# Closing residual sum and RMSNorm of a diffusion trunk: the sums on VectorE alone, Ln and Exp per pair of tiles, three tiles scaled by GpSimd

## The reference, cut to what matters

```python
def rmsnorm(x, g):
    xf = x.astype(jnp.float32)
    y = xf * lax.rsqrt(jnp.mean(xf * xf, axis=-1, keepdims=True) + EPS)
    return (y * g.astype(jnp.float32)).astype(x.dtype)

# expert_choice_ffn
ys = jnp.einsum('becf,efd->becd', hid, w_down) * gates[..., None].astype(h.dtype)
return jnp.zeros_like(h).at[bidx, idx].add(ys)

# trunk_layer, its last step
x = x + gate2 * expert_choice_ffn(h, router_w, exp_w_gate, exp_w_up, exp_w_down)

# at the end
y_prompt = rmsnorm(xp, final_norm_g)
y_sample = rmsnorm(xs, final_norm_g)
```

## Time and profile before

| what | value |
|---|---|
| median of three executions | 2427.76 us (2424.95 to 2427.86) |
| the profiled execution's own time | 2428.42 us |
| its span in the trace | 2426.7 us |
| PE busy | 2327.6 us (96%) |
| DVE busy | 1107.5 us (46%) |
| ACT busy | 937.2 us (39%) |
| POOL busy | 379.9 us (16%), 267 instructions |
| granted TensorE clock, mean | 0.984 |

### The profile page before, as it was taken

One profiled execution on the slowest core, in us unless ns is written; L12 is line 12 of the kernel. 1 busy time (PEld: TensorE's weight loads), 2 busy tenths in 40 slices (PEclk: granted clock), 3 DMA queues, 4 the chain that ended last, 5 costly groups with the idle time before them and its releaser, 6 DMA issues.

```text
span 2426.7 us, 39841 instructions
## 1 busy us (share of the span) xinstructions
PE 2327.6 (96%) x14256; PEld 1695.5 (70%) x14256; DVE 1107.5 (46%) x2161; ACT 937.2 (39%) x2447; POOL 379.9 (16%) x267
## 2 busy tenths in 40 slices
PE   6989999999999999999999999679999999999998
PEld 3456666575656565665644444579999999999996
DVE  2577786868686776766235317710010001000013
ACT  3164646556473747454311133213222322223213
POOL 0241313223140314132100000000010100110010
PEclk8999999999999999999999999889999999999999
DMA  9521212020211112121442422458778887888874
GB/s 343 219 58 38 69 37 68 17 88 18 64 42 41 56 28 68 28 69 40 149 169 95 143 89 94 161 211 295 267 251 282 291 296 241 270 287 294 283 233 159
DMA packets 198403, 361.06 MB, mean 149 GB/s; under 512 B 8955, under 2 KB 72328, under 8 KB 195244
## 3 DMA queue, kind: packets, MB, share of 16 engines
q1 hardware_dynamic: 192139, 341.77, 40.3%
q0 software_dynamic: 6176, 18.29, 3.0%
HBM read 319.97 MB, written 40.06 MB: 148 GB/s over the span
## 4 chain that ended last, share of the span: by engine, by line
PE 86%; DVE 5%; issue 3%; ACT 3%; DMA 2%; DVEq 0%; SPq 0%; ACTq 0%; POOL 0%; POOLq 0%
PE bank L757 22%; PE bank L2426 21%; PE bank L2440 11%; PE bank L2055 5%; PE bank L1792 5%; PE bank L957 3%; PE bank L1810 2%; PE bank L735 2%; PE bank L949 2%; PE bank L1015 2%; PE bank L1026 1%; PE bank L1031 1%; DMA arena<-in_ada_w 1%; PE bank L743 1%; PE bank L1030 1%
## 5 line engine op out<-in xcount | busy, mean ns | idle before, releaser
L757 PE MATMUL bank<-arena 128*128 128x512 f32 x1344 | 678.1, 608 | 2.8 <-ACT arena L791 2.8
L2426 PE MATMUL bank<-arena 128*128 128x144 f32 x4096 | 513.1, 286 | 3.1 <-ACT arena L2474 3.1
L2426 PEld LDWEIGHTS bank<-arena 128*128 128x128 f32 x4096 | 509.8, 190 | 3.2 <-ACT arena L2474 3.2
L2541 DVE TENSOR_TENSOR arena<-arena,bank 128x144 f32<-128x144 f32 x128 | 39.2, 306 | 700.2 <-ACT arena L2488 700.2
L757 PEld LDWEIGHTS bank<-arena 128*128 128x128 f32 x1344 | 217.8, 191 | 91.9 <-issue 87.5
L2440 PE MATMUL bank<-arena 128*128 128x144 f32 x2048 | 257.3, 286 | 0.7 <-DVE arena L2541 0.7
L2440 PEld LDWEIGHTS bank<-arena 128*128 128x128 f32 x2048 | 253.8, 189 | 1.9 <-DVE arena L2541 0.9
L2488 ACT ACTIVATE arena<-bank 128x144 f32<-128x144 f32 x128 | 37.5, 293 | 464.4 <-PE bank L2426 464.4
L957 PEld LDWEIGHTS bank<-arena 128*128 128x128 f16 x1296 | 96.4, 98 | 156.0 <-issue 137.4
L1135 ACT ACTIVATE arena<-bank 128x384 f16<-128x384 f16 (+1 forms) x360 | 159.4, 490 | 92.1 <-PE bank L957 67.5
L791 ACT ACTIVATE arena<-bank 128x128 f32<-128x128 f32 (+1 forms) x156 | 75.9, 491 | 172.4 <-PE bank L757 107.9
(11 more groups left out here) (309 smaller groups left out, 3213.5 us busy)
## 6 DMA issues: line engine op xcount, KB each, us to landing
arena<-in_exp_w_gate SPq DMA_DIRECT2D x32, 2048.0 KB, 10.0
arena<-in_exp_w_up SPq DMA_DIRECT2D x32, 2048.0 KB, 15.0
arena<-in_exp_w_down SPq DMA_DIRECT2D x32, 2048.0 KB, 10.8
arena<-in_w_in SPq DMA_DIRECT2D x52, 512.0 KB, 5.3
arena<-in_ada_w SPq DMA_DIRECT2D x24, 1024.0 KB, 7.9
side_dram<-arena SPq DMA_DIRECT2D x20, 576.0 KB, 4.4
arena<-g_dram SPq DMA_DIRECT2D x16, 576.0 KB, 4.1
arena<-in_x_sample SPq DMA_DIRECT2D x16, 512.0 KB, 7.2
```

The source lines that it names most:

```text
L757: ins = nc.tensor.matmul(bank[:, 0:LH], w[:, k, :], x[:, k, :], start=(k == 0 and job[2] in "127"), stop=(k == KH - 1), skip_group_check=( ...
L2426: last = nc.tensor.matmul(banks[3 + f % 2][:, m * CAP:(m + 1) * CAP], w_unit[2 * half + m][:, k, col:col + P], xsT[:, k, :], start=(k == 0 ...
```

## The change

1. `BY_TENSOR` goes. All nine sums are made by VectorE; TensorE has no identity matmuls left in this stage (L2460, 8 of its 48 matmul rows of this stage), ScalarE no copies from PSUM.
2. Ln and Exp run once per group of `LAST_GROUPS` = (0,1), (2,3), (4,5), (6,7), (8), over one or two columns, after the Squares of the whole group; `rstd2` counts groups. ScalarE also waits for its own previous step before each Square.
3. VectorE's order is: the sums of a group, then the scales of the group before it.
4. Tiles 1, 3 and 6 (`BY_POOL`) are scaled by GpSimd in two operations, a tensor_scalar with `frs` and then a tensor_tensor with `fin_row`, with a wait for the first between them. The stores of these tiles wait for GpSimd; the order of the stores stays.

```diff
@@ pe9
-            whole = i in BY_TENSOR
-            if whole:
-                pe.wait_ge(sem(f"tile_in{i}"), 16 + 16)
-                for half in range(2):
-                    nc.tensor.matmul(pair[half][:, 0:512], ident, xf[i][:, half * 512:(half + 1) * 512], start=True, stop=False)
...
-                    last = nc.tensor.matmul(pair[half][:, 0:512], place_l[:, i - 1, :], ys_l[:, half * 512:(half + 1) * 512], start=not whole, stop=True)
+                    last = nc.tensor.matmul(pair[half][:, 0:512], place_l[:, i - 1, :], ys_l[:, half * 512:(half + 1) * 512], start=True, stop=True)
-    BY_TENSOR = (2, 5)
+    LAST_GROUPS = ((0, 1), (2, 3), (4, 5), (6, 7), (8,))
+    BY_POOL = (1, 3, 6)
@@ sync10
-            sp.wait_ge(sem("yf_ready"), t + 1)
+            if t in BY_POOL:
+                sp.wait_ge(sem(f"tile_in{t}"), 16 + 16 + 2)
+            else:
+                sp.wait_ge(sem("yf_ready"), t + 1 - sum(b < t for b in BY_POOL))
@@ act10
+        for group in LAST_GROUPS:
+            at, to = group[0], group[-1] + 1
+            for t in group:
+                act.wait_ge(sem("x_summed"), t + 1)
+                act.wait_ge(sem("act_step"), n)
+                nc.scalar.activation(sqf, xf[t], ACT.Square, accum_out=fss[:, t:t + 1]).then_inc(sem("act_step"), 1)
+                n += 1
+            act.wait_ge(sem("act_step"), n)
+            nc.scalar.activation(fln[:, at:to], fss[:, at:to], ACT.Ln, scale=1.0 / D, bias=eps_c).then_inc(sem("act_step"), 1)
             n += 1
             act.wait_ge(sem("act_step"), n)
+            nc.scalar.activation(frs[:, at:to], fln[:, at:to], ACT.Exp, scale=-0.5).then_inc(sem("rstd2"), 1)
@@ dve10
-        def scale(t):
-            dve.wait_ge(sem("rstd2"), NT + t + 1)
-            nc.vector.scalar_tensor_tensor(xf[t], xf[t], frs[:, t:t + 1], fin_row, ALU.mult, ALU.mult).then_inc(sem("yf_ready"), 1)
...
+        def scale(n):
+            dve.wait_ge(sem("rstd2"), NT + n + 1)
+            for t in LAST_GROUPS[n]:
+                if t not in BY_POOL:
+                    nc.vector.scalar_tensor_tensor(xf[t], xf[t], frs[:, t:t + 1], fin_row, ALU.mult, ALU.mult).then_inc(sem("yf_ready"), 1)
+
+        for n, group in enumerate(LAST_GROUPS):
+            for t in group:
+                add(t)
+            if n > 0:
+                scale(n - 1)
+        scale(len(LAST_GROUPS) - 1)
+
+    def pool10(pool):
+        pool.wait_ge(sem("rows_in"), ROWS_ALL + 16)
+        for n, group in enumerate(LAST_GROUPS):
+            pool.wait_ge(sem("rstd2"), NT + n + 1)
+            for t in group:
+                if t in BY_POOL:
+                    pool.wait_ge(sem(f"tile_in{t}"), 16 + 16)
+                    nc.gpsimd.tensor_scalar(xf[t], xf[t], frs[:, t:t + 1], None, ALU.mult).then_inc(sem(f"tile_in{t}"), 1)
+                    pool.wait_ge(sem(f"tile_in{t}"), 16 + 16 + 1)
+                    nc.gpsimd.tensor_tensor(xf[t], xf[t], fin_row, ALU.mult).then_inc(sem(f"tile_in{t}"), 1)
```

More of the change, by code:

```diff
@@ L2608, in act10 @@
         n = ACT_PRO + 2 * NT
[L2609 to L2616, removed]
+        for group in LAST_GROUPS:
[7 more added lines that the diff above has]
+            nc.scalar.activation(fln[:, at:to], fss[:, at:to], ACT.Ln, scale=1.0 / D, bias=eps_c).then_inc(sem("act_step"), 1)
             n += 1
-            nc.scalar.activation(sqf, xf[t], ACT.Square, accum_out=fss[:, t:t + 1]).then_inc(sem("act_step"), 1)
             act.wait_ge(sem("act_step"), n)
[L2620 to L2623, removed]
+            nc.scalar.activation(frs[:, at:to], fln[:, at:to], ACT.Exp, scale=-0.5).then_inc(sem("rstd2"), 1)
     def dve10(dve):
@@ L2628, in add @@
         def add(t):
-            if t in BY_TENSOR:
-                return
             dve.wait_ge(sem(f"tile_in{t}"), 16 + 16)
             dve.wait_ge(sem("y_filled"), NT + t + 1)
-            if t - 1 in BY_TENSOR:
-                dve.wait_ge(sem("x_summed"), t)
             pair = PAIRS[t % len(PAIRS)]
@@ L2699, in f_pool @@
             pool9(pool)
+            pool10(pool)
     return {"sync": f_sync, "tensor": f_pe, "scalar": f_act, "vector": f_dve, "gpsimd": f_pool}
```

## The result

The changed kernel took 2429.76 us in the median of 18 runs (2428.0 to 2433.84), the kernel before 2426.71 us in the median of its 18 (2424.95 to 2429.72). The ratio is 1.0015, with a 95% interval of 1.0008 to 1.0021: a small loss of 3.1 us, with an interval of 1.9 to 5.1 us. The 3.1 us lie inside the 0.2%, or 4.9 us, that was called no change. The profiled execution of the changed kernel took 2430.77 us with a span of 2429.1 us, 2.4 us over the span before.

What follows compares the result with a forecast made beforehand. The closing stage was taken as bound by VectorE's sums and scales, with contention from GpSimd deciding. The middle of plus 1.3 and plus 2.8 us, plus 2.0, on a base of 2427.8 gave 2429.8 us, range 2425.0 to 2433.2.

Steps and rivals of the forecast that it cites:

- signs written down for a wrong forecast: Closing stage: a scale at 1.28 us across a GpSimd operation, a tensor_scalar over 2 us, or tile 6 stored after VectorE's last scale.
- Without contention VectorE would end at 2420.4: VectorE's new order with nothing held: scale 8 runs from 2419.1 to 2420.4, 3.1 us ahead of before.
- Sums go free, GpSimd's operations and scales exclude each other: Port rule: VectorE's scales and GpSimd's operations block each other for their full length; sums from PSUM are not held.
- The tensor_scalar takes 1.1 us: GpSimd's first operation per tile, 1024 columns: 1.1 us, taken nearest to the affine_selects.
- The end that I kept, 3.1: Upper end for GpSimd's tensor_scalar: the one row of 1.55 us for 512 columns, doubled to 3.1 us.
- two estimates of 0.9 and 2.2 us: GpSimd's operations with one and two inputs over 1024 elements, by the Trainium skill's cycles per element at 1.2 GHz.
- Scale 0 held by 1.9 us, scale 2 by 0.9, then scale 7 or 8 by 2.2: VectorE's scales behind GpSimd's operations: scale 0 1.9 us late, scale 2 2.8 us late in all, scale 8 ending at 2424.7 or 2424.8.
- the second rival: GpSimd slower than taken: with a 3.1 us tensor_scalar, stores pile up, plus 6.9 us, 2434.7; chance 0.23.
- The first to start wins, scales 4 and 5 run before GpSimd gets its turn: Order on the port: scales 4 and 5 run until 2418.9, and only then tile 6's tensor_scalar, to 2419.9.
- The stores of 6, 7 and 8 pile up if GpSimd is second: If scale 7 beats tile 6's tensor_tensor, the stores land 1.28 us apart, the last at 2428.9: 2.8 us later.
- the other (plus 1.3): If tile 6's tensor_tensor beats scale 7, scale 8 ends at 2424.7 and the last store lands at 2427.4, 1.3 us later.
- The gain on TensorE is only a bound: TensorE fills tile 8 at 2413.7 instead of 2417.2, 3.4 us, counting only as long as VectorE waits for TensorE.

Runs made afterwards that it cites:

- e8: Changed kernel without GpSimd's tensor_tensor, tiles 1, 3 and 6 stored without the gains; one execution, VectorE ends 22.6 us after TensorE's first placing matmul.
- e2: Changed kernel with the gains copied to PSUM for VectorE's scales, done in two halves, and three bank pairs for sums; ratio to the kernel before 1.0001.
- e4: Kernel before plus, after its last store, thirteen probes of GpSimd operations alone or beside VectorE's scales or sums; tensor_scalar alone 2.85 us, tensor_tensor alone 2.34 us.
- e7: Changed kernel without GpSimd's tensor_scalar, tiles 1, 3 and 6 stored without 1/rms; one execution, VectorE ends 23.5 us after TensorE's first placing matmul.
- e9: Changed kernel with the stores of tiles 6 and 7 exchanged; last packet at 29.2 us after TensorE's first placing matmul, ratio to the kernel before 1.0006.
- e3: Kernel before with BY_TENSOR empty, so VectorE makes all sums, nothing else changed; ratio to the kernel before 1.0004, VectorE ends at 25.0 us.
- e1: Changed kernel with BY_POOL empty, so all sums and scales on VectorE in the new order; ratio to the kernel before 0.9999, VectorE ends at 25.5 us.
- e10: Changed kernel with tile 6 scaled by VectorE again, GpSimd keeping tiles 1 and 3; ratio to the kernel before 0.9999, VectorE ends at 25.3 us.

## Why the prediction was right, point by point

The number was right, and so was the core of the mechanism: scales held behind GpSimd, and stores piled up behind tile 6. But the steps that led to it were wrong in the length of the tensor_scalar, in what it holds, in who wins and so in which scales are held, and they cancelled. That they did was luck. Two of the signs written down for a wrong forecast came true, a scale at 1.28 us across a GpSimd operation (tile 0) and a tensor_scalar over 2 us, and the scales of tiles 0 and 2 took 1.28 and 1.37 us, not 3.1 and 2.2.

That 2429.8 met 2429.76 is luck as well. The change was forecast as plus 2.0 us and measured as plus 3.1; the base, 2427.8 from three executions, was 1.1 us above the 2426.71 of eighteen.

- *Without contention VectorE would end at 2420.4.* Right: e8, with no scale held, ends 22.6 us after the first placing matmul, which is 2420.4.
- *Sums go free, GpSimd's operations and scales exclude each other.* Right for the sums and, once it has got its turn, for the tensor_tensor (e2, e4, e7). Wrong for the tensor_scalar, which in e4 held a scale only for about its first microsecond.
- *The tensor_scalar takes 1.1 us.* Wrong, the mis-sized term: 2.85 alone. The affine_selects were the wrong neighbour, and of the row with 1.55 us for 512 columns I took a part for waiting, where it is the plain cost (1.57 in e4). The end that I kept, 3.1, was nearly it. Two of the three took 3.81 us, with 1.0 us of waiting for a scale. (The prediction's two estimates of 0.9 and 2.2 us lie 0.35 us below its own 3.45 in all, not 0.2 to 0.3.)
- *Scale 0 held by 1.9 us, scale 2 by 0.9, then scale 7 or 8 by 2.2.* Wrong in place: held were the scales of tiles 5 and 8, by 2.1 and 2.0, and that of tile 2 by 0.1. The sum, 4.2 us, was nearly the 4.3 by which these steps move 2420.4 (they add to 5.0, of which 0.7 goes into the wait for the last Exp), and VectorE ended at 2424.5 for 2424.7 predicted. With a tensor_scalar near its right length (3.1) and the wrong rule that it holds all along I would have had plus 6.9 us, the second rival. The two errors together gave the right sum.
- *The first to start wins, scales 4 and 5 run before GpSimd gets its turn.* Wrong: GpSimd, waiting, goes in between two scales, and about 0.4 us after the start of its record a scale could still overtake it (e4).
- *The stores of 6, 7 and 8 pile up if GpSimd is second.* Right, with the landing at 2428.9 predicted and 2428.7 measured; e9 gives 1.3 us for it. GpSimd was second not because two starts within 0.1 us fell that way, but because tile 6's tensor_scalar ended only at 2421.0. The forecast of plus 2.0 was the middle between this case (plus 2.8) and the other (plus 1.3).
- *The gain on TensorE is only a bound.* Right in the sense that VectorE set the end; the parts that the prediction had not separated are minus 0.7 us for the sums (e3) and plus 0.5 for the groups (e1 against e3). GpSimd's share is plus 1.2 at VectorE's end (three scales fewer, minus 3.6; 0.6 of waiting for the last Exp; 4.1 of holds) and 1.3 for the pile.

Together that is 2.3 us more to the last packet in the profiles (30.5 against 28.2). The medians differ by 3.1 and the ratio's interval holds 1.9 to 5.1, so a part of up to 2.8 us outside this stage is neither shown nor excluded. e10 speaks against a large one: it has the same new order and GpSimd's two operations on two tiles, its last packet comes at 28.2 as in the kernel before, and its ratio is 0.9999 (0.999 to 1.0008).

## What to carry to other kernels

Work given to GpSimd can come back as waiting on VectorE if both read two large operands from SBUF: count for each GpSimd tensor_tensor the VectorE instruction that it holds, or move one operand of VectorE's instruction to PSUM. Price GpSimd's operations by the same operation in the trace, even if there is only one row of it. If results leave in a fixed order, a late tile from the slow engine delays the stores of all behind it.

## What the runs showed of the hardware that was not expected

- GpSimd's tensor_scalar over 128x1024 f32 (one large operand) took 2.85 us, its tensor_tensor (two) 2.34 us. The spacing of the records agrees: in e2 each tensor_tensor starts 2.9 us after its tensor_scalar. The estimate worked out from the Trainium skill's figure for one input (GPSIMD Engine Reference, "Performance versus the Vector engine"), 0.9 us, is a third of what was measured.
- The Trainium skill (SBUF — State Buffer, "Who interferes with whom") has the port held for the whole instruction. In e4 the tensor_tensor does that once a scale comes 1.45 us into it (1.98 us for a scale of 1.17), but a scale 0.37 us into it went first. The tensor_scalar doesn't (1.29 and 1.16 us, from 0.9 and 1.4 us into it); it held the second of two scales for about 0.8 us.
- A GpSimd instruction that waits while a scale runs gets its turn before the next scale, though the two scales follow each other without a gap (3.36 us for the second, in the changed kernel).
